# A norm seam's first rounded half: from ScalarE behind the residual to VectorE ahead of it, with 10 warm-up products for 13

## The reference, cut to what matters

```python
def rms_norm(x, g):
    xf = x.astype(jnp.float32)
    y = xf * lax.rsqrt(jnp.mean(xf * xf, axis=-1, keepdims=True) + RMS_EPS)
    return (y * g.astype(jnp.float32)).astype(x.dtype)
...
        h = h + rms_norm(y, mix_norm_post[layer])
        f = swiglu(rms_norm(h, ffn_norm_pre[layer]), ffn_w_gate_up[layer], ffn_w_down[layer])
```

## Time and profile before

| | |
|---|---|
| median of the runs | 2037.16 us |
| the profiled execution's own time | 2037.03 us |
| its span in the profile | 2035.2 us |
| TensorE busy | 2012.8 us, 99% |
| VectorE busy | 1475.5 us, 72% |
| ScalarE busy | 908.7 us, 45% |
| granted clock of TensorE, mean | 0.997 |
| warm-up products in seams (L2043) | 65, 5 times 13 |

### The profile page before, as it was taken

How to read it: one execution, slowest core, us unless ns; L and a number is a source line. 1 busy time by engine, 2 the same in 40 slices (tenths; PEclk the granted TensorE clock), 3 DMA queues, 4 the chain that set the end, 5 groups by cost and what they waited for, 6 DMA issues and landing times.

```text
span 2035.2 us, 31849 instructions
## 1 busy us (share of the span) xinstructions
PE 2012.8 (99%) x12178; PEld 1775.9 (87%) x12178; DVE 1475.5 (72%) x2458; ACT 908.7 (45%) x1601; POOL 9.7 (0%) x23
## 2 busy tenths in 40 slices
PE   9999999999999999999999999999999999999998
PEld 7888899988889898898897899998888778999887
DVE  6646999843784766757757899973488979999534
ACT  4225555532623323323334665542343576555323
POOL 0000000000000000000000000000000000000000
PEclk9999999999999999999999999999999999999999
DMA  5862422232125142151241222233222123323421
GB/s 183 118 116 83 145 104 103 103 145 96 70 103 146 63 115 91 65 145 63 75 133 63 104 104 104 103 110 138 103 95 73 63 104 104 111 99 115 150 84 62
DMA packets 43451, 211.36 MB, mean 104 GB/s; under 512 B 4007, under 2 KB 7112, under 8 KB 21976
## 3 DMA queue, kind: packets, MB, share of 16 engines
q1 hardware_dynamic: 29008, 181.48, 24.9%
q10 hardware_dynamic: 13416, 25.81, 4.7%
q0 software_dynamic: 928, 2.70, 2.6%
HBM read 187.43 MB, written 9.96 MB: 97 GB/s over the span
## 4 chain that ended last, share of the span: by engine, by line
PE 93%; DVE 3%; ACT 2%; issue 1%; DMA 0%; DVEq 0%; ACTq 0%; SPq 0%
PE bank L1991 52%; PE bank L2113 27%; PE bank L2034 5%; PE bank L2378 2%; PE bank L2336 2%; PE bank L2354 1%; PE bank L2023 1%; DVE c L1806 1%; DVE work L1171 1%; PE bank L2523 0%; PE bank L2395 0%; ACT w_hi L618 0%; PE bank L2548 0%; DVE work L1236 0%; DVE h L1239 0%
## 5 line engine op out<-in xcount | busy, mean ns | idle before, releaser
L1132 DVE TENSOR_TENSOR w_lo<-w_raw,w_hi 128x2048 fp32r<-128x2048 f32 (+1 forms) x95 | 178.0, 1884 | 237.2 <-ACT w_hi L618 237.2
L618 ACT ACTIVATE w_hi<-w_raw 128x2048 fp32r<-128x2048 f32 (+1 forms) x81 | 148.0, 1828 | 355.4 <-PE bank L1991 315.1
L1991 PE MATMUL bank<-x_hi,w_hi 128*128 128x512 f32 x704 | 284.4, 404 | 0.0
L1991 PE MATMUL bank<-x_hi,w_lo 128*128 128x512 f32 x704 | 274.9, 390 | 0.0
L1991 PE MATMUL bank<-x_lo,w_hi 128*128 128x512 f32 x704 | 274.3, 390 | 0.0
L2113 PE MATMUL bank<-form_hi,f_hi 128*128 128x256 f32 x864 | 244.7, 283 | 1.9 <-ACT kept L753 1.9
L2113 PE MATMUL bank<-form_lo,f_hi 128*128 128x256 f32 x864 | 244.5, 283 | 0.0
L2113 PE MATMUL bank<-form_hi,f_lo 128*128 128x256 f32 x864 | 244.5, 283 | 0.0
L1991 PE MATMUL bank<-ring_hi,w_hi 128*128 128x512 f32 (+1 forms) x542 | 208.1, 384 | 0.0
L1991 PE MATMUL bank<-ring_lo,w_hi 128*128 128x512 f32 (+1 forms) x542 | 207.9, 384 | 0.0
L1991 PE MATMUL bank<-ring_hi,w_lo 128*128 128x512 f32 (+1 forms) x542 | 207.9, 384 | 0.0
(11 more groups left out here) (256 smaller groups left out, 4234.0 us busy)
## 6 DMA issues: line engine op xcount, KB each, us to landing
w_raw<-w_all SPq DMA_DIRECT2D x167, 1024.0 KB, 4.8
qk<-qk_next ACTq DMA_DIRECT2D x32, 384.0 KB, 10.9
h_save<-h ACTq DMA_DIRECT2D x3, 2048.0 KB, 12.5
h<-h_save ACTq DMA_DIRECT2D x3, 2048.0 KB, 8.6
w_raw<-w_all SPq DMA_DIRECT2D x6, 256.0 KB, 6.8
h<-x_t SPq DMA_DIRECT2D x3, 512.0 KB, 7.8
skew<-erow POOLq DMA_DIRECT2D x8, 192.0 KB, 8.7
out_t<-h SPq DMA_DIRECT2D x3, 512.0 KB, 3.0
```

Of the source, the lines that this page charges most:

```text
L618: ins = nc.scalar.activation(w_hi[slot(u)][:, part], w_raw[u % 2][:, part], ACT.Copy, scale=1.0 if g is None else g)
L1132: ins = v.tensor_tensor(w_lo[p][:, part], raw, hi, ALU.subtract)
L1991: ins = mm(out, b if flip else a, a if flip else b, start=start and n == 0, stop=stop and n == 2, **kw)
```

## The change

In seams 1, 3, 4 and 5, ScalarE makes two products of 256 tokens ahead of time, just before its square of block 0: first_y = y * post gain (in seam 5 from PSUM) and first_h = h * pre gain. When the factor of the first half is there, VectorE makes first_t = first_y * pre gain * factor and rounds x_hi = first_t + first_h, both before it begins with the residual of block 0. In seam 2, which has no pre gain, it reads y and h themselves and ScalarE makes nothing. ScalarE no longer rounds the first half of block 0 in these seams. TensorE waits for the factor of the second half (`yr_ready`) ahead of its first products, and issues 10 warm-up products instead of 13.

```diff
-WARM = 13
+WARM = 10
...
+        first_y, first_h, first_t = work[:, 4, HALVES[0]], work[:, 4, HALVES[1]], work[:, 3, HALVES[1]]
...
                     square = bank[bank_of_y(t, m)] if m in IN_PSUM[t] else y[:, m, :]
+                    if t != 2 and m == 0:
+
+                        nc.scalar.activation(first_y, square[:, HALVES[0]], ACT.Copy, scale=gain(POST_GAIN[t]))
+                        nc.scalar.activation(first_h, h[:, 0, HALVES[0]], ACT.Copy,
+                                             scale=gain(PRE_GAIN[t])).then_inc(first_gained, 1)
                     for c in [slice(0, S)] if i < KC - 1 else HALVES:
...
             def pre_norm(t):
 
-                for hf in range(2):
-                    act.wait_ge(h_ready, blocks_ready(t, 0) - 1 + hf)
-                    pre_norm_hi(t, 0, HALVES[hf])
+                act.wait_ge(h_ready, blocks_ready(t, 0))
+                pre_norm_hi(t, 0, HALVES[1])
...
+            def first_hi(t):
+
+                c = HALVES[0]
+                if t == 2:
+                    src, g, base = y[:, 0, c], gain(POST_GAIN[t]), h[:, 0, c]
+                else:
+                    dve.wait_ge(first_gained, t if t == 1 else t - 1)
+                    src, g, base = first_y, gain(PRE_GAIN[t]), first_h
+                order.link(v.scalar_tensor_tensor(first_t, src, g, work[:, RQ, c], ALU.mult, ALU.mult))
+                v.tensor_tensor(x_hi[:, 0, c], first_t, base, ALU.add).then_inc(xhi_done, 1)
+
             def transition(t):
...
-                for hf in range(2):
-                    dve.wait_ge(yr_ready, 2 * t - 1 + hf)
-                    residual(t, 0, HALVES[hf])
+                dve.wait_ge(yr_ready, 2 * t - 1)
+                first_hi(t)
+                residual(t, 0, HALVES[0])
+                dve.wait_ge(yr_ready, 2 * t)
+                residual(t, 0, HALVES[1])
...
                 pe.wait_ge(w_split, u + 2)
+                pe.wait_ge(yr_ready, 2 * t)
                 for hf in range(2):
                     pe.wait_ge(xhi_done, rounded_count(t, 0) - 1 + hf)
```

More of the change, by code:

```diff
@@ L421, in program @@
         yr_ready = sem("yr_ready")
+        first_gained = sem("first_gained")
         h_ready = sem("h_ready")
```

## The result

The changed kernel took **2042.56 us** (median of 8 runs, 2038.97 to 2044.95) against 2037.24 us (8 runs, 2034.87 to 2038.82) of the kernel before on the same chip: a ratio of 1.0028, 95% interval 1.0019 to 1.0036, so 3.9 to 7.3 us slower. The forecast was 2042.3, slower.

The account below looks back on a forecast made before the run. TensorE holds 93% of the chain, but block 1's rounding, led by VectorE's list, was taken to end each seam. Terms 3.44 + 0.18 + 1.6 = 5.2 us over the kernel before gave 2042.3 us, range 2040.0 to 2045.0.

Parts of the forecast that it names:

- What sets the seam: End of each seam: set by when block 1 is rounded, led by VectorE's list without a hole, not by block 0.
- the distances: From VectorE's first operation of a seam to block 1's first product: 4.86 us instead of 4.00; seam 3's stays.
- The warm-up products: Ahead of block 0: 3 fewer free 0.49 us of TensorE per seam, booked at nothing, covered by the wait for block 1.
- The chain of seam 2: Warm-up products run straight into block 0; ground for a rival: 0.49 us won per seam, 2.4 in all, 2034.7; 5%.
- the 0.22 us of the earlier trace: Seam 2 of the kernel before: TensorE's wait on the rounding of block 1, seen in the timeline.
- The two VectorE operations: Head of VectorE's list: block 1 starts 0.86 us later in seams 1, 2, 4 and 5, 3.44 us together.
- seam 3 at nothing: Seam 3: VectorE stands idle 0.78 us for the second factor, whose lateness covers the two new operations.
- ScalarE's products ahead of the sums: Before block 0's square: two copies delay adds and sums by 0.54, 0.13, 0.42, 0.51 in seams 1, 3, 4, 5; 1.6 us.
- The row of 0.41 us: Profile row: seven ScalarE copies with a gain per partition, 256 wide, took 2.89 us, 0.41 each, so 0.82 for two.
- The extra wait of VectorE's sequencer: Wait for `first_gained` ahead of VectorE's first operation: 0.06 us in each of three seams, 0.18 us.
- Rival C: Slower still: TensorE's clock falls in a seam where it waits; 2043.8 with one seam, 2048.1 with four; 11%.
- my sum from rows 11: Behind 1117.60: 8 products at the 1.2 GHz level would have taken 1.95 us at full clock, so 1.45 us lost.

Follow-up runs that it names:

- e4: Changed kernel with VectorE's residual of block 0's first half moved behind block 1's, ScalarE's square of block 0 moved to fit; ratio 1.0015 to the kernel before.
- e5: Changed kernel with VectorE's two new operations of each seam done twice; ratio 1.0048 to the kernel before.
- e2: Kernel before with 10 warm-up products instead of 13, nothing else; ratio 1.0002 to the kernel before.
- e3: Changed kernel with 13 warm-up products again instead of 10; ratio 1.0030 to the kernel before.
- e1: Kernel before with ScalarE's two products added ahead of the square of block 0 (seams 1, 3, 4, 5), read by nobody; 2039.54 us, ratio 1.0012.
- e7: Kernel before with 11 warm-up products and block 1's x_hi rounded by VectorE instead of ScalarE; 2032.38 us, ratio 0.9984.
- e6: Changed kernel without ScalarE's two products, VectorE reading y and h themselves in all seams; ratio 1.0015 to the kernel before.

## Why the prediction was right

**What sets the seam.** Block 1's rounding, through VectorE's list. Shown by the distances (4.86 forecast, 4.85 measured), by e4 (the list back in order for block 1: 4.00 again) and by e5 (doubling the pair: once more in every seam).

**The warm-up products at nothing.** e2 at 1.0002 and e3, with the same 4.85 as the changed kernel, both show it. The chain of seam 2 spoke for 0.49 us a seam and was misleading: a product's recorded end can hide a short wait (in seam 1 of before four half-width products are recorded as 0.64 us and the next four start 0.48 behind them, 187.65 to 188.13); the 0.22 us of the earlier trace rows was the true sign.

**The two VectorE operations, 3.44 forecast.** 3.39 measured, and seam 3 at nothing, for the reason given.

**ScalarE's products ahead of the sums, 1.6 forecast.** 1.50 in the changed kernel's trace: 0.52, 0.13, 0.41 and 0.44 for 0.54, 0.13, 0.42 and 0.51. Seam 5 was sized 0.07 too high. Seam 3's 0.13 is there in the changed kernel, e4 and e5 (0.65, 0.66, 0.64) and not in e1 and e3, which have the products too (0.52 as before). The timelines tell the two apart. In the changed kernel the second square ends at 1122.49 + 0.52 + 0.63 = 1123.64 and the add follows at once, as my working had it:

```profile
1122.49 2.18 ACT L659 ACTIVATE y_sq<-y 128x512 f32<-128x512 f32 x4
...
1123.66 0.69 DVE L1227 TENSOR_TENSOR y_sq<-y_sq 128x512 f32<-128x512 f32 x1
```

In e1 the clock is at 0.50 until 1124.14 (in e3 from 1121.60 to 1125.01), while the last rows of the product fill the banks, and VectorE's copies wait for TensorE:

```profile
1123.57 0.69 DVE L1221 TENSOR_TENSOR y<-part,bank 128x512 f32<-128x512 f32 x1 [0.52 <-PE bank L1995]
```

There the second square ends at 1125.04 and the add starts only at 1125.91, behind VectorE's own copies, so the two products are hidden. The working for seam 3 was right for an execution whose clock is not low while those banks fill.

The row of 0.41 us from one such copy to the next held: in the changed kernel's timeline they start 0.40 apart at 0.50 each. The estimate from the Trainium skill, "ScalarE: Activation LUTs", Rules for kernel authors, 0.51 us for 256 elements, fits the duration of one and not the distance of two.

**The extra wait of VectorE's sequencer, 0.18 forecast.** From the first sum to VectorE's first operation it is 2.13 us in seam 1 in both kernels (182.75 to 184.88; 183.07 to 185.20). It costs nothing. The sum of the parts is therefore 4.9 and not 5.2. (My terms add up to 5.22, which over 2037.16 gives 2042.4 and not 2042.3.) That the median came out within 0.3 us of the forecast is luck: the parts were 0.3 too high, and the interval of the measured loss is 3.4 us wide.

**The clock.** Rival C is not seen: there is no fall between the last product ahead of a seam and its last block in any profile, the changed kernel, e3, e4 and e5 among them, though TensorE waits in these four for up to 0.81 us between the halves and again for block 1. What I had left out is that the clock falls outside the seams in some executions and not in others, and that one fall is 1.35 us (1.45 by my sum from rows 11). The executions of the kernel before differ by up to 5.0 us (28 runs beside e1 to e4), those of the changed kernel by up to 6.0, as much as the effect itself. The 5.3 us between the medians and the 4.9 of the trace both lie within 3.9 to 7.3. At the same mean clock of 0.999 the shortest runs are 2033.76 (one of those 28, so not taken beside the changed kernel) and 2038.97, 5.2 us apart.

## What to carry to other kernels

When a stage is fed by an engine that works through a list, ask which item of the list the consumer is truly waiting for; here it was the second block, and making the first one ready sooner by putting work at the head of the list only turned one wait into a longer one. Work that is "made ahead of time" has to be placed against its own queue: two copies of 0.4 us each, put before a square that an add waits for, delayed the sums by 0.4 to 0.5 us in three seams. A chain of waits that runs through a busy engine does not prove that the engine is the limit; look for short waits right behind it. And look at each place by itself: e7 gains in four seams and hardly in seam 2, where the list that was made longer became the limit itself.

## What the runs showed that I had not expected

- The clock fell at about the same places (from 607 to 611 us and from 1117 to 1122 us of the span on) in some executions and not in others: twice in the profiled execution of before, in e1's and e3's, once in e2's and e7's, three times in e6's (a third one at 1607 us), and not at all in those of the changed kernel, e4 and e5, up to the last 4 to 6 us of the span, where every profile has 0.50. These are different kernels; that executions of one kernel differ in this is known only from their mean clocks (0.996 to 0.999 for the changed one). The first place is behind 16 products of a single column; TensorE counts as busy there in the record, and the clock still fell.
- With TensorE waiting 0.81 us and 0.39 us within 2.5 us of a seam the granted clock stayed at 1.00, as in this stretch of the changed kernel:

```profile
187.40:190.10 2.70, 1.51 (x12) 1.09 (x10) 2.64 (x5) 1.86 (x4) 0.00 (x0) 1.00 0.43 182
```

- In seam 4 of the kernel before, a square of ScalarE started 0.33 us after what it waits for, and in e6 and e7 the wait ahead of that seam's sum was 0.09 us instead of 0.20. No run here says why.
